# Log decays and small projections made inside the input projection of a gated mixer, and the gated stage's first tiles loaded early

## The reference

```
proj = h @ w_in                          # 1024 x 14368
# branch A, 8 heads of 128 keys
z = a_f                                  # 1024 columns
log_f_a = log_sigmoid(z)                 # the lower bound lb is 0 for one layer
k_a = sigmoid(-z);  q_a = silu(a_q)
o_a = gated_linear_attention(q_a, k_a, a_i, log_f_a)
# branch B, 4 heads of 128 keys, 256 values
gk = b_gk @ gla_w_gk + gla_b_gk          # b_gk: 16 columns, w: 16 x 512
log_f_b = log_sigmoid(gk) / 16
o_b = gated_linear_attention(b_q * 128**-0.5, b_k, b_v, log_f_b)
# branch C: qkv = silu(causal_short_conv(c_qkv, gdn_conv)), 3072 columns, four taps
#           log_a, beta from c_a, c_b (8 columns each); gated_delta_rule(...)
```

## Time and profile before

| | |
|---|---|
| runs | 4485.14, 4490.4, 4484.26 us; median 4485.14 |
| the profiled execution | 4486.69 us, of which the span is 4484.8 us |
| mean granted TensorE clock | 0.963 |
| PE busy | 4049.8 us (90%), 25919 instructions |
| PEld busy | 3157.4 us (70%) |
| DVE busy | 2740.2 us (61%) |
| ACT busy | 1827.1 us (41%) |
| POOL busy | 783.6 us (17%) |
| DMA | 522.10 MB, mean 116 GB/s |

### The profile page before, as it was taken

One profiled execution on the slowest core, in us unless ns is written; L12 is line 12 of the kernel. 1 busy time (PEld: TensorE's weight loads), 2 busy tenths in 40 slices (PEclk: granted clock), 3 DMA queues, 4 the chain that ended last, 5 costly groups with the idle time before them and its releaser, 6 DMA issues. The chain is left out here.

```text
span 4484.8 us, 65698 instructions
## 1 busy us (share of the span) xinstructions
PE 4049.8 (90%) x25919; PEld 3157.4 (70%) x25919; DVE 2740.2 (61%) x3542; ACT 1827.1 (41%) x3361; POOL 783.6 (17%) x855
## 2 busy tenths in 40 slices
PE   8999889979988988999999999688869968999997
PEld 1788667668866767788887787466558854788786
DVE  1413677751167766555567776488746656756789
ACT  0312466531136543322223443487645523433533
POOL 0200400020040002000200300276523312222001
PEclk9999999989999999999999999699989989999998
DMA  7534421124332114233344443222132147234332
GB/s 264 174 108 159 140 74 50 50 108 161 112 138 80 38 43 142 93 104 122 104 146 145 168 147 127 81 68 81 63 131 77 45 173 290 82 103 150 113 122 80
DMA packets 266929, 522.10 MB, mean 116 GB/s; under 512 B 35160, under 2 KB 71352, under 8 KB 266380
## 3 DMA queue, kind: packets, MB, share of 16 engines
q1 hardware_dynamic: 266640, 518.15, 33.0%
HBM read 365.30 MB, written 152.78 MB: 116 GB/s over the span
## 5 line engine op out<-in xcount | busy, mean ns | idle before, releaser
L958 ACT CAST p_th<-spare 128x1024 fp32r<-128x1024 f32 x156 | 163.7, 1050 | 533.4 <-PE p_ps L910 533.4
L1107 DVE TENSOR_TENSOR p_tl<-spare,p_th 128x1024 fp32r<-128x1024 f32 x156 | 196.8, 1266 | 277.6 <-ACT p_th L958 277.3
L314 PE MATMUL p_ps<-p_wh,hi 128*128 128x512 f32 x896 | 352.5, 393 | 6.6 <-DVE p_wl L482 6.6
L314 PE MATMUL p_ps<-p_wh,lo 128*128 128x512 f32 x896 | 350.5, 391 | 0.0
L314 PE MATMUL p_ps<-p_wl,hi 128*128 128x512 f32 x896 | 350.5, 391 | 0.0
L910 PE MATMUL p_ps<-p_th,p_xh 128*128 128x512 f32 x784 | 307.2, 392 | 15.5 <-DVE p_tl L1107 15.5
L910 PE MATMUL p_ps<-p_tl,p_xh 128*128 128x512 f32 x784 | 305.7, 390 | 0.0
L910 PE MATMUL p_ps<-p_th,p_xl 128*128 128x512 f32 x784 | 305.7, 390 | 0.0
L910 PE MATMUL p_ps<-p_xh,p_th 128*128 128x512 f32 x672 | 262.3, 390 | 2.9 <-DVE p_tl L1107 2.9
L910 PE MATMUL p_ps<-p_xh,p_tl 128*128 128x512 f32 x672 | 261.7, 389 | 0.0
L910 PE MATMUL p_ps<-p_xl,p_th 128*128 128x512 f32 x672 | 261.6, 389 | 0.0
(11 more groups left out here) (487 smaller groups left out, 10511.4 us busy)
## 6 DMA issues: line engine op xcount, KB each, us to landing
spare<-w_in SPq DMA_DIRECT2D x56, 1024.0 KB, 5.4
p_raw<-w_in SPq DMA_DIRECT2D x40, 1024.0 KB, 5.9
pn_dram<-p_stg SPq DMA_DIRECT2D x128, 256.0 KB, 2.1
p_dram<-p_stg SPq DMA_DIRECT2D x112, 256.0 KB, 2.0
m_w<-w_mod SPq DMA_DIRECT2D x12, 2048.0 KB, 12.6
pt_dram<-p_stg SPq DMA_DIRECT2D x96, 256.0 KB, 2.2
zm_ogm<-pn_dram SPq DMA_DIRECT2D x48, 512.0 KB, 10.3
zu_raw<-w_up SPq DMA_DIRECT2D x16, 1024.0 KB, 5.4
```

Source lines behind the costliest of these rows:

```text
L314: mm = pe.matmul(ps[:, u, :], lhsT, rhs, start=(kk == 0 and q == 0), stop=(kk == KD - 1 and q == 2))
L958: act.copy(th[:, g % 2], (R11, T, R21, R12, R22, R11, R21)[i][:, 2 * u:2 * u + 2]).then_inc(s_hi, 1)
L1107: dve.tensor_tensor(tl[:, g % 2], (R11, T, R21, R12, R22, R11, R21)[i][:, 2 * u:2 * u + 2], th[:, g % 2], ALU.subtract).then_inc(s_lo, 1)
```

## The change

Five things are done:

1. The small projections become part of `seven_products`, in group 0: PE's `decay_logits(0)` and `(1)` after the first units of i = 0 and 1, `turn_ab` after that of i = 2; ACT takes the logits into staging tiles, SP stores them to DRAM. `small_projections` goes, and so does the round trip of `low_dram`.
2. Twelve **key jobs** are added to `seven_products`, at p = 6, 9 of group 2, all four spots of groups 3 and 4, and p = 0, 3 of group 5: SP loads the logits of a head, ACT Abs and Exp in iteration g and Ln in g + 1, DVE log decay and key logits in g + 1, ACT the keys in g + 2, SP stores both and loads the next.
3. The tap jobs of odd units (p = 3, 9) have their DVE part moved to iteration g + 1.
4. The gated stage loads log decays and keys ready made; its Abs, Exp, Ln, key Exp and the two DVE steps go. `take_decay` moves ahead of the output copy in ACT's order, `decay_rest` to j = 1 on DVE.
5. SP loads the log decays of heads 0 and 1 and the first queries and keys during the last group, into parts of `spare` that the weight blocks have left.

```diff
+        logit_q = next(q for q in range(NQ) if groups[q]["keys"] is not None)
+        keys_at = {UN * q + p: n for n, (q, p) in enumerate([(q, p) for q in range(logit_q + 1, NQ) for p in (0, 3, 6, 9)][2:2 + A_HEADS + B_HEADS])}
+            def load_logits(n):
+                if n == 0:
...
+                elif n <= A_HEADS:
+                    sp.wait_ge(s_kst, 16 * n)
+                else:
+                    sp.wait_ge(s_lt, n)
+                sp.dma_start(z, logits(n)).then_inc(s_zl, 16)
+            def store_keys(q, p):
...
+                sp.wait_ge(s_lt, n + 1)
+                sp.dma_start(logits(n), cv[:]).then_inc(s_lst, 16)
+                if n < A_HEADS:
+                    sp.wait_ge(s_k, n + 1)
+                    sp.dma_start(heads(groups[logit_q]["keys"], n), z).then_inc(s_kst, 16)
+                if n + 1 < A_HEADS + B_HEADS:
+                    load_logits(n + 1)
...
-            sp.wait_ge(s_eA, 2 * NB // 2 + 2)
-            sp.dma_start(C.low_dram, cv[0:2 * RANK, :]).then_inc(s_low, 16)
+            for n in range(2 * B_HEADS):
+                h, c = n // B_HEADS, n % B_HEADS
+                sp.wait_ge(s_gk, n + 1)
+                sp.dma_start(C.pt_dram[T_BF + c * P:T_BF + (c + 1) * P, h * CH:(h + 1) * CH], stg[:, n % SG, :]).then_inc(s_st[n % SG], 16)
             for q in range(NQ):
                 for i, freed in ((2, ((1, 8), (3, 10))), (4, ((0, 12),)), (5, ((2, 14),)), (6, ())):
...
                     for p in {2: (0, 3), 4: (6,), 5: (9,), 6: ()}[i]:
+                        store_keys(q, p)
                         store_rows(q, p)
...
+                        elif b == 1:
+                            sp.wait_ge(s_lo, UN * q + units)
+                            for n in range(2):
+                                sp.dma_start(C.g_lt[:, n], heads(C.pt_dram[T_AF:T_AF + 2 * P, :], n)).then_inc(C.s_lt_in[n], 16)
+                        elif b == 0:
+                            sp.wait_ge(s_lo, UN * q + units)
+                            sp.dma_start(C.g_q0, C.pt_dram[T_AQ:T_AQ + P, :]).then_inc(C.s_in[0], 16)
+                            sp.dma_start(C.g_k0, C.pt_dram[T_AK:T_AK + P, :]).then_inc(C.s_in[0], 16)
...
+            def decay_logits(h):
...
+                    pe.matmul(ps[:, 4 * (1 - h) + c, :], C.wg[:, c * P:(c + 1) * P], low, start=True, stop=True).then_inc(s_pg, 1)
+            def turn_ab():
+                pe.wait_ge(s_C, added[1] + 1)
+                for t in range(NT):
+                    mm = pe.transpose(ps[:, 4, ...], C.low[0:2 * RANK, t * P:(t + 1) * P], ...)
...
                         if u == 0:
                             mm.then_inc(s_u0, 1)
+                            if q == 0 and i < 2:
+                                decay_logits(i)
+                            elif q == 0 and i == 2:
+                                turn_ab()
...
+            def log_term(n, step):
+                if step == 0:
+                    act.wait_ge(s_zl, 16 * (n + 1))
...
+                        act.wait_ge(s_lst, 16 * n)
+                        if n <= A_HEADS:
+                            act.wait_ge(s_kz, n)
+                    act.activation(cv[:], z, ACT.Abs)
+                    act.drain()
+                    act.activation(cv[:], cv[:], ACT.Exp, scale=-1.0)
+                else:
+                    act.drain()
+                    act.activation(cv[:], cv[:], ACT.Ln, bias=1.0).then_inc(s_ln, 1)
+            def keys(n):
+                act.wait_ge(s_kz, n + 1)
+                act.activation(z, z, ACT.Exp).then_inc(s_k, 1)
...
                 unit_hi(g + 2)
                 if g - 2 in job_at:
                     rows_activated(job_at[g - 2])
+                if g - 1 in keys_at:
+                    log_term(keys_at[g - 1], 1)
+                if keys_at.get(g - 2, A_HEADS) < A_HEADS:
+                    keys(keys_at[g - 2])
...
                 if g in job_at:
                     first_tap(job_at[g])
+                if g in keys_at:
+                    log_term(keys_at[g], 0)
+                if g in (0, 2):
+                    for c in range(B_HEADS):
...
+                        act.activation(stg[:, n % SG, :], ps[:, 4 * (1 - g // 2) + c, :], ACT.Identity, bias=C.bg[:, c:c + 1]).then_inc(s_gk, 1)
...
+            def log_decay(n):
+                dve.wait_ge(s_ln, n + 1)
+                dve.scalar_tensor_tensor(cv[:], z, 0.0, cv[:], ALU.min, ALU.subtract).then_inc(s_lt, 1)
+                if n < A_HEADS:
+                    dve.drain()
+                    dve.tensor_tensor(z, cv[:], z, ALU.subtract).then_inc(s_kz, 1)
...
-                if g in job_at:
+                if g in job_at and u == 0:
                     other_taps(job_at[g])
+                if g - 1 in job_at and u == 0:
+                    other_taps(job_at[g - 1])
+                if g - 1 in keys_at:
+                    log_decay(keys_at[g - 1])
...
@@ gated_linear, sync @@
-            load_z(0)
             sp.dma_start(sums[:], ins["t_decay"]).then_inc(s_tab, 16)
-            load(0)
-            load_z(1)
             sp.dma_start(masks[:], ins["t_levels64"]).then_inc(s_tab, 16)
             load_v(0)
             load(1)
-            load_z(2)
+            load_lt(2)
...
@@ gated_linear, scalar @@
-            for step in range(3):
-                log_term(0, step)
             take_decay(0)
             for p in range(4):
                 exps(p)
-            queries_keys(0)
-            for step in range(3):
-                log_term(1, step)
             take_decay(1)
...
-            for i in range(4):
-                prepare(2, i)
             take_k(0)
...
+                for a, i in head_prep(m):
+                    if i == 5:
+                        take_decay(a)
                 act.wait_ge(s_o, m + 1)
```

More of the change, by code:

```diff
@@ L699, in seven_products @@
         spots = [(q, p) for q in range(conv_q[0] + 1, NQ) for p in (0, 3, 6, 9)][2:2 + JOBS]
+        logit_q = next(q for q in range(NQ) if groups[q]["keys"] is not None)
+        keys_at = {UN * q + p: n for n, (q, p) in enumerate([(q, p) for q in range(logit_q + 1, NQ) for p in (0, 3, 6, 9)][2:2 + A_HEADS + B_HEADS])}
+        logits = lambda n: heads(groups[logit_q]["out"], n) if n < A_HEADS else heads(C.pt_dram[T_BF:T_BF + B_HEADS * P, :], n - A_HEADS)
+        heads = lambda ap, n: ap[n * P:(n + 1) * P, :]
+        z = rows[:, PAD:]
         job_at = {UN * q + p: n for n, (q, p) in enumerate(spots)}
@@ L778, in load_rows @@
                 sp.dma_start(rows[:, PAD:], r[n % C_HEADS * P:(n % C_HEADS + 1) * P, :]).then_inc(s_rl, 16)
+            def load_logits(n):
+                if n == 0:
+                    for b in range(SG):
+                        sp.wait_ge(s_st[b], 16 * ((PLAIN + 16 * (logit_q + 1)) // SG))
+                    sp.wait_ge(s_nl, 1)
+                    sp.wait_ge(s_n, 2)
+                elif n <= A_HEADS:
[4 more added lines that the diff above has]
+            def store_keys(q, p):
+                n = keys_at.get(UN * q + p)
+                if n is None:
+                    return
+                sp.wait_ge(s_lt, n + 1)
[5 more added lines that the diff above has]
+                    load_logits(n + 1)
             def store_rows(q, p):
@@ L1027, in _ @@
                     first_tap(job_at[g])
+                if g in keys_at:
+                    log_term(keys_at[g], 0)
+                if g in (0, 2):
+                    for c in range(B_HEADS):
+                        n = B_HEADS * (g // 2) + c
+                        act.wait_ge(s_pg, n + 1)
+                        act.wait_ge(s_st[n % SG], 16 * ((2 * NB + n) // SG))
+                        act.activation(stg[:, n % SG, :], ps[:, 4 * (1 - g // 2) + c, :], ACT.Identity, bias=C.bg[:, c:c + 1]).then_inc(s_gk, 1)
         @block.gpsimd
@@ L2106, in gated_linear @@
     half_of = lambda m: m // HP
-    in_loads = [16 * (n // 3 + 1) + 16 * sum(1 for j in range(n % 3, n + 1, 3) if not first(j)) for n in range(H)]
+    in_loads = [32 * (n // 3 + 1) for n in range(H)]
     with ExitStack() as st:
@@ L2140, in gated_linear @@
         s_tab = sem("tables_loaded")
-        s_z = [sem(f"logits_loaded{b}") for b in range(2)]
-        s_in = [sem(f"head_loaded{b}") for b in range(3)]
+        s_lt_in, s_in = C.s_lt_in, C.s_in
         s_v = [sem(f"values_loaded{b}") for b in range(2)]
@@ L2225, in _ @@
             load(1)
-            load_z(2)
+            load_lt(2)
             load(2)
             load_v(1)
-            load_z(3)
+            load_lt(3)
             for n in range(H):
-                if first(n + 4):
-                    load_z(n + 4)
+                if n + 4 < H:
+                    load_lt(n + 4)
                 if n + 3 < H:
@@ L2242, in _, with queries @@
         def _(act):
[L2243 to L2265 removed]
+            def queries(n):
+                b = n % 3
+                act.wait_ge(s_in[b], in_loads[n])
+                act.mul(q[b], q[b], float(P) ** -0.5).then_inc(s_q, 1)
```

(23 more changed lines are left out.)

178 lines of the change are left out of this document (64 added, 114 removed).

## The result

The changed kernel took 4416.2 us, median of four runs (4415.6 to 4427.6), against 4487.4 (4484.3 to 4490.4) for the one before: ratio 0.9847, interval [0.983, 0.9865]. It is 71 us faster; 4410 was forecast. Repeated later on two chips it gave 0.9845 [0.9831, 0.9858] and 0.984 [0.9827, 0.9854].

A forecast was written before the change was run, and what follows sets the result against it. PE bounds the input projection, the order of work within a chunk the gated stage. Terms -16.2 + 7.7 - 10 + 5 - 25 - 37 = -75.5 take the profiled 4486.7 to 4411.2, median 4410 us; range 4393 to 4437.

The forecast's parts named there:

- seam: Between input projection and gated stage: the separate stage of small projections goes whole, -16.2 us.
- start: Gated stage's start: first output about +32 us after its first DMA, before +57.6; gain -25, ends -18 and -28.
- taps: Input projection: taps behind the split remove PE's p = 3 waits, p = 9 waits move two units on; -10 us.
- small projections: Input projection, group 0: eight matmuls and eight transposes return on PE, +7.7 us; ends 0 and +15.3.
- key jobs: Input projection: p = 9 jobs miss unit 14's split in groups 2 to 4; sum +5 us, ends 0 and +24.
- chunks: Gated stage's chunks: a head of A falls from 29.1 to about 25.0 us; -37 in all, ends -24 and -43.
- Rival D: Between the stages: the seam stays, early loads save nothing, only chunks and taps count; near 4450 us; chance 0.02.
- +23.3: Gated stage's start: POOL's second half at +23.3 us from the stage's first DMA, before +41.9.
- Rival A: Input projection: key jobs' round trips stall PE 2 to 3 us per job, +24 to +36, about 4435; chance 0.15.
- Rival C: Input projection: SP's single order makes weight blocks late, whole pipeline shifts; slower, 4515 at 9 us per job; chance 0.03.
- The pair of 8.26: Gated stage, head of A: two slow chunks taking 8.26 us together fall to about 6.8, -1.5 per head.
- rival B: Gated stage: DVE or POOL sets the head at 26.5 us; -24 for -37, with slower start 4425; chance 0.17.

The follow-up runs named there:

- the repeat: The changed kernel run and profiled once more, nothing altered: 4414.4 us, ratio 0.9845 to the kernel before.
- The late loads: Changed kernel with first log decays, queries and keys loaded at the gated stage's start again, in the order of before: 4422.6 us, ratio 0.9844.
- the first profile: Profile of the changed kernel's first profiled execution, the longest of its four runs: 4427.6 us.

## Why the prediction was right, and where its terms were off

The forecast, 4410, is 6 us under the median, and for the most part the total is right for its own reasons: seam and start within 1 us, taps within 1 to 1.5, small projections and key jobs off by 2 and 1 against each other (in the repeat), and the chunks 4 to 6 short. Some of the nearness is luck: the changed stages gave 66 and 70 us in the two profiles for 75.5, and in the repeat 2.4 came from stages that nobody touched.

- **Seam (-16.2) and start (-25)**: -41.2 forecast for both, -40.4 and -40.9 measured. Rival D is out. The steps inside were off against each other: tables at +3.3, not +5; POOL at +13.9, not +15.5. But "+23.3" for POOL's second half could not be: before, its first half already took 2883.94 - 4.18 - 2869.09 = 10.7 us, so the second half can't start before +26. It did no harm, since the first output hangs on the first half. The late loads show what the early ones gave: 7 us, as the two tables land earlier by as much.
- **Taps (-10)**: -10.8 to -11.5 shown by the taps put back, and the four waits moved two units on with 8.2 us before and 8.1 after, as the text had it.
- **Key jobs (+5)**: 3.8, clock included. The stalls came where they were looked for, by the chain that the text has (Ln late, then log decay, joins and split), but smaller: 0.7 to 0.9 us in group 3 instead of 1.4, 1.4 more than before in group 4 instead of 2, and none in group 2. Rival A's mechanism is in it with one stall of the twelve jobs: the round trips cost ACT up to 3.8 us of waiting, of which PE felt what went beyond 3.0. Rival C's mechanism did not begin: ACT has no wait for a weight block's DMA in any of these groups.
- **Small projections (+7.7)**: the term that was mis-sized. The matmuls took 3.72 for four and 0.7 for the transposes, 8.1 in all, but the clock fell to half at their end or behind them. In the repeat (one spell of 3.4) that is 1.7 more, 9.8; in the first profile (two of 6.8, the second four taking 4.92 themselves) group 0 took 5.1 more still, 14.9, next to the upper end of 15.3. That end had been put down to half clock in the small matmuls; most of it went in the full products behind them.
- **Chunks (-37)**: -31 to -33. ACT's load, Ln and load were worth 2.24 per head (forecast 2.2). The pair of 8.26 should have fallen to 6.8; there are 6.9 to 7.8 in fact, two chunks further on, and the four chunks that hold both places take 12.5 to 13.5 for 14.3 before: it is no longer ACT that is late but DVE, beside POOL. That is rival B's mechanism in two chunks of eight; its price was 4 to 6 us, not 13. The sign of being right, no chunk but the turn's above 3.3, did not come. The moved order, which the forecast took as a part of 1.5 us per head, is worth 19 us over the stage once the key steps are gone, half of it through the clock. Order (19) and table loads with Ln (16) together exceed the 31 to 33 that the stage won, so they can't be added; how they overlap was not tried.

## What to carry to other kernels

When preparation leaves a chunk loop, look at the order in which the remaining steps stand, not only at the load that goes: here the same steps in the old order cost 19 us, where the stage had won 31 to 33. A step that is short alone can be long beside its neighbour: price it by its longest row beside the engine it shares with, and move the shortest such step to another engine (the copy of 128x8 on ACT gave 5 us). And small matmuls put between full ones on a PE-bound path cost their own time, and four in a row the clock behind them as well.

## What the runs showed of the hardware

- A 16x512 f32 matmul between products takes 0.93 us in a row of four and 1.14 alone. At the end of four in a row or just behind, with PE never idle, the granted clock went to 0.50 for 3.4 or 6.8 us, in ten profiles out of ten (14 of 20 rows of four); with single ones between full products it stayed at 1.00 in three out of three. What it is about the four that lowers the clock was not taken apart.
- DVE and POOL: a copy of 128x8 takes 0.17 us with POOL idle and up to 1.51 beside it, a product of two 128x512 tiles 0.69 and up to 1.39. POOL's half of twelve products takes 10.5 us with four of DVE's factors in it (the first half after the change) and 8.7 with none (the second); in the heads, with one or two, 8.8 to 9.4. The Trainium skill, "SBUF — State Buffer", section "SBUF: two separate sides", says that VectorE with two SBUF inputs, or in a two-port mode, and GpSimd take a port pair in turn, for a whole instruction. The trace agrees: products that read PSUM (the mask, 0.61 to 0.63) did not change beside POOL.
